# Relative bias of the MoBA attention: one 96-column product per key set with the table's three bf16 parts side by side, in place of three 32-column products

## The reference, cut to what matters

```python
def t5_bucket(dist):                      # 32 buckets over dist = pos_query - pos_key
    ...
def rel_bias(pq, pk):
    return table_h[h_i4, t5_bucket(pq - pk)].astype(jnp.float32)    # table: 32 buckets x 8 heads
lg_own = (einsum('bhqd,bhtd->bhqt', qi, k_own) * scale + rel_bias(pq4, pos_own[:, None, None, :]))
```

## Time and profile before

| what | value |
|---|---|
| device time, median of 3 runs (range) | 922.52 us (921.96 to 923.47) |
| profiled execution: span from first to last instruction | 920.4 us |
| median time less that span | 2.1 us |
| mean granted TensorE clock | 0.991 |
| PE busy | 892.8 us, 97% |
| PE weight loads busy | 774.4 us, 84% |
| VectorE (DVE) busy | 623.8 us, 68% |
| ScalarE (ACT) busy | 525.5 us, 57% |
| chain that ended last, share of PE | 88% |
| HBM read | 140.77 MB |

### The profile page before, as it was taken

One profiled execution on the slowest core, in us unless ns is written; L12 is line 12 of the kernel. 1 busy time (PEld: TensorE's weight loads), 2 busy tenths in 40 slices (PEclk: granted clock), 3 DMA queues, 4 the chain that ended last, 5 costly groups with the idle time before them and its releaser, 6 DMA issues.

```text
span 920.4 us, 13095 instructions
## 1 busy us (share of the span) xinstructions
PE 892.8 (97%) x5254; PEld 774.4 (84%) x5254; DVE 623.8 (68%) x1033; ACT 525.5 (57%) x848; POOL 78.3 (9%) x96
## 2 busy tenths in 40 slices
PE   6899999999999999999999999999999999999997
PEld 6777888888888888888888888999988888798885
DVE  6887686756666576657655556696786666776775
ACT  5788644435444686636444434565546565657782
POOL 0055000000000000000000000002535312000000
PEclk9999999999999999999999999999999799999999
DMA  8442456535554544447555654555430041654411
GB/s 261 138 150 81 138 183 245 187 137 184 201 195 153 183 137 141 150 153 242 179 189 175 222 197 139 182 160 166 138 101 37 5 157 46 203 190 180 165 65 46
DMA packets 61677, 142.67 MB, mean 155 GB/s; under 512 B 5296, under 2 KB 7344, under 8 KB 61616
## 3 DMA queue, kind: packets, MB, share of 16 engines
q1 hardware_dynamic: 61616, 141.83, 45.3%
HBM read 140.77 MB, written 1.05 MB: 154 GB/s over the span
## 4 chain that ended last, share of the span: by engine, by line
PE 88%; DVE 4%; POOL 3%; issue 2%; ACT 1%; SPq 1%; DMA 0%; DVEq 0%; POOLq 0%; ACTq 0%
PE ps L491 85%; PE ps L499 4%; POOL arena L3525 3%; SPq L3617 1%; DVE wlo L2309 1%; DVE sub L2309 1%; ACT arena L1376 0%; ACT whi L1376 0%; DVE xhl L2309 0%; POOL otl L3525 0%; DMA pint<-rel_bias_table_dram 0%; DVE arena L2309 0%; DVE X L2309 0%; DVE arena L2315 0%; ACT otl L1376 0%
## 5 line engine op out<-in xcount | busy, mean ns | idle before, releaser
L2309 DVE TENSOR_TENSOR wlo<-raw,whi 128x2048 fp32r<-128x2048 f32 (+3 forms) x130 | 286.8, 2214 | 121.7 <-ACT whi L1376 121.5
L1376 ACT ACTIVATE whi<-raw 128x2048 fp32r<-128x2048 f32 (+3 forms) x136 | 250.8, 1852 | 178.7 <-PE ps L491 166.7
L491 PE MATMUL ps<-xhl,whi 128*128 128x512 f32 (+3 forms) x928 | 257.7, 348 | 0.0
L491 PE MATMUL ps<-xhl,wlo 128*128 128x256 f32 x720 | 202.5, 281 | 0.0
L491 PEld LDWEIGHTS ps<-xhl,whi 128*128 128x128 f32 (+2 forms) x928 | 158.9, 186 | 25.0
L491 PE MATMUL ps<-whi,xhl 128*128 128x512 f32 (+2 forms) x528 | 168.9, 388 | 1.9 <-DVE xhl L2315 1.7
L491 PE MATMUL ps<-whi,oth 128*128 128x512 f32 x416 | 164.8, 396 | 0.2 <-DVE otl L2315 0.2
L491 PE MATMUL ps<-whi,otl 128*128 128x512 f32 x416 | 162.4, 390 | 0.0
L491 PE MATMUL ps<-wlo,oth 128*128 128x512 f32 x416 | 162.1, 390 | 0.0
L491 PEld LDWEIGHTS ps<-xhl,wlo 128*128 128x128 f32 x720 | 134.9, 187 | 0.8
L491 PEld LDWEIGHTS ps<-whi,xhl 128*128 128x128 f32 x528 | 99.2, 190 | 18.9 <-DVE wlo L2309 3.2
(11 more groups left out here) (146 smaller groups left out, 880.9 us busy)
## 6 DMA issues: line engine op xcount, KB each, us to landing
raw<-mlp_w_in_dram SPq DMA_DIRECT2D x32, 1024.0 KB, 5.2
raw<-mlp_w_out_dram SPq DMA_DIRECT2D x32, 1024.0 KB, 5.0
raw<-gdn_w_in_dram SPq DMA_DIRECT2D x16, 1024.0 KB, 5.3
raw<-moba_w_qkv_dram SPq DMA_DIRECT2D x12, 1024.0 KB, 5.2
raw<-kv_w_dram SPq DMA_DIRECT2D x8, 1024.0 KB, 5.4
raw<-fox_w_in_dram SPq DMA_DIRECT2D x8, 1024.0 KB, 5.2
raw<-mla_w_o_dram SPq DMA_DIRECT2D x4, 1024.0 KB, 5.4
raw<-moba_w_o_dram SPq DMA_DIRECT2D x4, 1024.0 KB, 5.9
```

The lines of the kernel that those rows point to most:

```text
L491: return eng.matmul(o, l, r, start=start, stop=True, skip_group_check=True)
L1376: return eng.activation(o, i, f, **kw)
L2309: return eng.tensor_tensor(o, a, b, f)
```

## The change

Groups 0 to 2 stay as they are. From group 3 on a key set is one matmul of 96 columns that writes the three parts side by side, 4 key sets to a bank, so that a group is 8 matmuls in two banks taken one after the other from the ring. VectorE adds mask and three parts, in three steps for each bank, each waiting for the one before it. The products of groups 5, 7, 9, 11 move from just behind their even neighbour to three quarters later, groups 6 and 10 two quarters later. VectorE's indicators, bias adds and some of `hidden`, `hidden_sum` and `lo` change places.

```diff
--- before.py
+++ after.py
@@ -311,7 +311,8 @@
         kn = view(A_AT + 256, 128, "p (t n) -> p t n", t=2)
         kp = view(A_AT, 256, "p (t n) -> p t n", t=2)
         k_tmp = view(A_AT + 384, 256, "p (a t n) -> p a t n", a=4, t=2)
-        tbl = pint[:, 0:48].bitcast(BF16).rearrange("p (a n) -> p a n", a=3)
+        tbl_row = pint[:, 0:48].bitcast(BF16)
+        tbl = tbl_row.rearrange("p (a n) -> p a n", a=3)
 
 
         class Att:
@@ -751,13 +752,22 @@
             def bias_mm(q_):
                 L.wait_ge(s_tb, 1)
                 L.wait_ge(s_ind, q_ + 1)
-                b = ring(("bias", q_), s_bs, q_ + 1)
                 iv = ind_view(q_)
-                for t in range(2 if q_ < 8 else 1):
-                    for g_ in range(4 if q_ < 8 else 8):
-                        for p_ in range(3):
-                            a = 128 * t + 32 * g_
-                            ins = mm(P[b][:, a:a + 32], iv[:, g_, 128 * t:128 * t + 128], tbl[:, p_, :], p_ == 0)
+                if q_ < BIAS_IN_MLA:
+                    b = ring(("bias", q_), s_bs, q_ + 1)
+                    for t in range(2):
+                        for g_ in range(4):
+                            for p_ in range(3):
+                                a = 128 * t + 32 * g_
+                                ins = mm(P[b][:, a:a + 32], iv[:, g_, 128 * t:128 * t + 128], tbl[:, p_, :], p_ == 0)
+                    ins.then_inc(s_bm, 1)
+                    return
+
+                for z in range(2):
+                    b = ring(("bias", q_, z), s_bs, q_ + 1)
+                    for g_ in range(4):
+                        key = iv[:, g_, 128 * z:128 * z + 128] if q_ < 8 else iv[:, 4 * z + g_, 0:128]
+                        ins = mm(P[b][:, 96 * g_:96 * g_ + 96], key, tbl_row, True)
                 ins.then_inc(s_bm, 1)
 
             def turn_c(i):
@@ -1058,15 +1068,19 @@
             bias_mm(3)
             to(22, 2)
             bias_mm(4)
+            to(23, 1)
             bias_mm(5)
-            to(26, 0)
+            to(26, 2)
             bias_mm(6)
+            to(27, 1)
             bias_mm(7)
             to(30, 2)
             bias_mm(8)
+            to(31, 1)
             bias_mm(9)
-            to(34, 0)
+            to(34, 2)
             bias_mm(10)
+            to(35, 1)
             bias_mm(11)
             to(45, 2)
             turn_x("moba", 0)
@@ -2459,13 +2473,22 @@
 
             def bias_add(q_):
                 L.wait_ge(s_bm, q_ + 1)
-                b = P[bank["bias", q_]]
-                for t in range(2 if q_ < 8 else 1):
-                    base, n, u = (128 * t, 4, 4 * q_) if q_ < 8 else (256, 8, 8 * (q_ - 8))
-                    d = biasM[:, :, base:base + 128].rearrange("p h (k g) -> p h k g", k=4)[:, :, :, u:u + n]
-                    s_ = b[:, 128 * t:128 * t + 32 * n].rearrange("p (g k h) -> p h k g", g=n, k=4)
-                    m_ = K("mask")[:, base:base + 128].rearrange("p (k g) -> p k g", k=4)[:, :, u:u + n]
-                    ins = tt(d, s_, bc(m_.unsqueeze(1), 1, 8), ALU.add)
+                for z in range(2):
+                    base, u = (128 * z, 4 * q_) if q_ < 8 else (256, 8 * (q_ - 8) + 4 * z)
+                    d = biasM[:, :, base:base + 128].rearrange("p h (k g) -> p h k g", k=4)[:, :, :, u:u + 4]
+                    m_ = K("mask")[:, base:base + 128].rearrange("p (k g) -> p k g", k=4)[:, :, u:u + 4]
+                    if q_ < BIAS_IN_MLA:
+                        s_ = P[bank["bias", q_]][:, 128 * z:128 * z + 128].rearrange("p (g k h) -> p h k g", g=4, k=4)
+                        ins = tt(d, s_, bc(m_.unsqueeze(1), 1, 8), ALU.add)
+                        continue
+
+                    s3 = P[bank["bias", q_, z]][:, 0:384].rearrange("p (g a n) -> p a g n", g=4, a=3)
+                    sp = [s3[:, a, :, :].rearrange("p g (k h) -> p h k g", k=4) for a in range(3)]
+                    L.step(tt(d, sp[0], bc(m_.unsqueeze(1), 1, 8), ALU.add))
+                    L.settle()
+                    L.step(tt(d, sp[1], d, ALU.add))
+                    L.settle()
+                    ins = tt(d, sp[2], d, ALU.add)
                 ins.then_inc(s_bs, 1)
 
             def mean_x(stage):
@@ -3045,10 +3068,10 @@
             hidden(0, 0, 0)
             hidden(0, 0, 1)
             hidden_sum(0, 1, 0)
-            bias_ind(5)
             hidden_sum(0, 1, 1)
             lo(19)
             lo(20)
+            bias_ind(5)
             hidden(0, 1, 0)
             hidden(0, 1, 1)
             bias_add(3)
@@ -3058,23 +3081,23 @@
             hidden_sum(0, 2, 0)
             hidden_sum(0, 2, 1)
             bias_add(4)
+            bias_ind(6)
+            lo(24)
             bias_add(5)
-            bias_ind(6)
             bias_ind(7)
-            lo(24)
             lo(25)
             lo(26)
             hidden(0, 2, 0)
             hidden(0, 2, 1)
             lo(27)
             hidden_sum(0, 3, 0)
+            hidden_sum(0, 3, 1)
+            bias_add(6)
             bias_ind(8)
-            hidden_sum(0, 3, 1)
-            bias_ind(9)
             lo(28)
             level_masks()
-            bias_add(6)
             bias_add(7)
+            bias_ind(9)
             lo(29)
             lo(30)
             hidden(0, 3, 0)
@@ -3083,21 +3106,21 @@
             hidden_sum(0, 4, 1)
             lo(31)
             lo(32)
+            bias_add(8)
+            bias_ind(10)
             lo(33)
             gain("moba")
-            bias_add(8)
+            hidden(0, 4, 0)
             bias_add(9)
-            hidden(0, 4, 0)
             lo(34)
-            bias_ind(10)
             bias_ind(11)
             hidden_sum(0, 5, 0)
-            bias_add(10)
             hidden(0, 4, 1)
             lo(35)
+            hidden_sum(0, 5, 1)
+            bias_add(10)
+            lo(36)
             bias_add(11)
-            lo(36)
-            hidden_sum(0, 5, 1)
             hidden(0, 5, 0)
             variance(0)
             lo(37)
```

## The result

The changed kernel takes 930.34 us (median of 4 runs, 927.83 to 931.67) where the kernel before takes 922.44 (921.96 to 923.47, 4 runs): ratio 1.0087, 95% interval 1.0071 to 1.0102. It is 7.9 us slower; 7.0 was forecast (929.5).

What follows compares the result with a forecast made beforehand. PE's instruction stream was taken to bound the first MLP. Products and exits -1.4, waits +1.5, +1.2 and +4.1, clock +1.6 gave +7.0 us: span 920.4 to 927.4, median 922.5 to 929.5 us, range 925.0 to 932.0.

Steps and rivals of the forecast that it cites:

- products: Groups 3 to 11 on PE: 72 products of 96 columns at 52 ns, 3.74 us in place of 5.49.
- exits from a bias set: PE leaving a bias set for the next matmul: 0.09 us each, nine exits (0.81 us) in place of five (0.45).
- wait 1: Group 3 at (18, 0): its second half needs bank 6, which VectorE's additions free only at 136.00; 1.5 us lost.
- wait 2: Quarter (32, 1) of pw chunk 32: bank 5 is held until bias_add(9) ends at 218.85; 1.2 us lost.
- wait 3: Group 10 at (34, 2): bank 7 needs the additions of hidden_sum(0, 5, 1), behind lo(35) on VectorE; 4.1 us lost.
- clock: Behind the long PE wait at group 10: granted clock falls to 0.50, dense matmuls lose some 1.6 us.
- What bounds: First MLP: only PE's instruction stream sets the time, and a shift there is passed on whole.
- VectorE: Bias adds: six per group in two chains of three, 1.72 us a group; 11 us more over nine groups.
- The other moves cost nothing: Remaining groups and moved VectorE work: banks free or additions done in time, so no loss on PE.
- Rival 1: All three PE waits as forecast but no fall of the clock: +5.4 us, 927.9 us; chance 0.32.
- The not-slower one: PE meets no closed bank, half 1's additions being early before groups 3 and 10: -1.4 us, 921.1 us; chance 0.05.
- Rival 2: Long wait at (34, 2) halves or the one at (32, 1) vanishes: +1.5 to +3.5, 924.0 to 926.0 us; chance 0.10.

Runs made afterwards that it cites:

- all three banks changed: Changed kernel with groups 3, 8 and 10 in banks 4 and 5, groups 9 and 11 in 6 and 7: 920.50 us, ratio 0.9987 against the kernel before.
- The same bank, its additions earlier: Changed kernel, ScalarE's half_copy(0, 5, 1) and hidden_hi(0, 4, 1) before hi(36), VectorE's hidden_sum(0, 5, 1) before hidden(0, 4, 1) and lo(35): 923.16 us, ratio 1.0011.

## Why the prediction was right, point by point

The stretch grew by 7.99 us. On PE's timeline it adds up so, with the forecast beside it. What a wait costs is counted from the start that was due to the start that came:

| part | forecast | measured |
|---|---|---|
| products | -1.75 | -2.45 |
| exits from a bias set | +0.36 | +0.68 |
| wait 1 | +1.5 | +1.53 (group 3 takes 1.87 us, an undisturbed group 0.34) |
| wait 2 | +1.2 | +1.47 (the two pw chunks 12.77 us, before 11.30) |
| wait 3 | +4.1 | +4.18 (12 matmuls and the wait 6.97 us, before 2.79) |
| clock | +1.6 | +2.6: group 10 +0.25, the 18 matmuls behind it +2.35 |
| sum | +7.0 | +8.0 |

The mechanism was right: three closed banks at their places, with their releasers, and the clock behind the longest. That the sum is off by the clock's 1.0 us alone is luck, though: the products gave 0.7 us more than forecast, and the exits and waits together cost 0.7 us more.

**What bounds.** That PE's stream sets the time and that a shift there is passed on whole held in every kernel: from the end of the first MLP to the second addition all that were traced take 108.95 to 108.97 us. Behind that addition they take 517.6 to 518.8, 518.7 both before and after the change.

**Products.** The step that took 12 ns on top of the columns from the 32-column row was off: a wide product takes 42 ns, not 52, so only 2 ns come on top of its columns, and the 12 ns couldn't be carried over. The formula of columns plus 2.5 ns that the prediction cites from the Trainium skill, "TensorE: Matmul & The Clock Gate", section "Back-to-back issue gap", gives 42.5 ns, and the trace agrees. The section gives it for single matmuls, though; for a stream in which every matmul has a weight load, as here, it has about 81 ns at 128 columns, and the 42 ns at 96 columns don't bear that out.

**Exits.** These were forecast at half their size. The 0.09 us was read off one gap. Two exits inside a pair of back chunks make 11.21 us out of 10.95 without any, 0.13 each, and only 0.04 where the bias stands at the pair's beginning. Spreading the groups thus cost 0.68 us, over a quarter of what the width gave.

**The waits.** All three were forecast at their place and with their releaser, the first and third to 0.1 us, the second 0.27 short. Of these, 0.12 are the bias adds of groups 8 and 9, each 0.06 longer than forecast, and 0.10 the first matmul behind the wait (221.02 to 221.35, 0.33 us to its successor, not 0.23). Bank by bank, the argument is shown by the bank changes and, for the third, by moving the additions. The idle times in brackets (1.35, 1.22, 4.07) are shorter than what the waits cost, because they count from the end of the last matmul: at 219.52 + 0.28 = 219.80, where its successor was due at 219.64.

**VectorE.** A group's adds take 1.79 us (213.47 to 215.26), forecast 1.72; over nine groups they cost no time of their own that shows once the banks are right.

**"The other moves cost nothing"** was wrong by 0.44 us, and the cause is on PE. `lo(35)` stands behind `hidden(0, 4, 1)`, which waits for ScalarE, as it did before, and it ends 6.2 us after the pw chunks in either order (234.09 less 227.94 before; 233.74 less 227.57 with all three banks changed). But before the change PE ran 48 bias products ahead of chunk 35, 1.21 us, and started it 6.8 us after the pw chunks, behind `lo(35)`. Now only group 10 stands ahead of it, 0.34 us, and PE gets there at 5.9. In the changed kernel the third wait hides this. It showed when that wait was gone.

**The clock** was rightly put into the likeliest case, from a gap of about that length in the earlier trace rows. This is the term that was sized too low: in that row the clock was back after 3.3 us, here 5.5 us of work ran at half clock. One trace couldn't show that the time at half clock varies: behind the very gap of the earlier trace rows it was 3.4 us in seven of the eleven traces and 6.8 in four. In the four traces with the long wait it was 6.8 us three times, at a price of 2.6 to 2.7 us, and 3.4 us once, at a price of 1.3. Rival 1, the same without the clock, is ruled out for the traced executions; the others were not traced.

**The other rivals.** The not-slower one needed the additions of half 1 to be 1.5 and 4.1 us earlier; one experiment put the latter there and that loss was gone, so its point of decision was right. Rival 2 had its sum wrong: at the lower bound of the adds, 1.3 us, the second wait would still be some 0.3 us long, and without it the sum would be +5.8 with the clock's fall and +4.2 without, not +1.5 to +3.5.

## What to carry to other kernels

When an instruction saves PE time but asks for one more buffer, list for every use which buffer it gets and when its last reader is done, in the written order of that reader's engine. A rotating ring hides such a collision: here the choice of banks for five groups decided between +8 and -1 us of the stretch. Count a wait on a dense PE from the start that was due, and add its aftermath, some microseconds at half clock if it is long. And when products leave PE's stream ahead of a chunk, ask whether the chunk's weights are ready that much earlier.

## What the runs showed of the hardware

- In the first MLP the granted clock fell to 0.50 at waits of 4.0 to 4.1 us in all four traces with one, and 0.6 us behind the end of one of 2.23 us, and never at those of 1.35 or 1.22 us. It stayed at 0.50 for 6.8 us in three of the five cases and for 3.4 us in two, at a price of 2.6 to 2.7 and of 1.3 to 1.6 us. The length of the wait alone doesn't settle it: in the trace of "The same bank, its additions earlier" the clock also fell at 21.0 us, in the MLA stage, 1.4 us behind the end of a wait of 1.56 us. At the same place the other ten traces have waits of 0.39 to 1.30 us and no fall.
- Bf16 products of 96 columns, each with its own weight load, start every 42 ns; those of 32 columns every 25 ns. Three times the columns cost 1.7 times the time.
- A bias set in the middle of float32 matmuls costs 0.13 us beyond its own products, and 0.04 where it stands at the beginning of the back chunks.
- Executions of the same kernel spread by some 4 us (920.4 to 924.8 for the kernel before over 17 runs), with mean clocks of 0.989 to 0.993. Part of it arises before the first MLP, with the 3.4 or 6.8 us at half clock behind the early gap. For changes of one microsecond the stretch between two fixed pieces of the chain was the better measure.
